# Out-projection of a decoder step as three fp32r products in place of one fp32 product

## The reference

```python
q, k, v, g = in_projection(rms_norm(yp, norm1_g[l]), w_in[l])
attn = merge_branches([banded_branch(q, k, v, dil, win // dil) for win, dil in DILATIONS])
c = conformer_conv(g_hist, conv_w[l], conv_b[l], conv_ln_g[l], conv_ln_b[l])
yp = yp + jnp.concatenate([attn.astype(yp.dtype), c], axis=-1) @ w_out[l]     # the out-projection
yp = channel_block(yp, norm2_g[l], w_query[l], sub_keys1[l], sub_keys2[l], expert_u[l], expert_v[l])
...
y_prompt = rms_norm(yp, final_g)
```

## Time and profile before

| what | value |
|---|---|
| median of 3 runs | 1710.42 us (1708.64 to 1710.57) |
| the profiled execution, its time | 1709.66 us |
| the profiled execution, its span | 1707.8 us |
| PE busy | 1645.9 us, 96% of the span |
| DVE busy | 1316.1 us, 77% |
| ACT busy | 618.3 us, 36% |
| mean granted TensorE clock | 0.99 of full |

### The profile page before, as it was taken

One profiled execution on the slowest core, in us unless ns is written; L12 is line 12 of the kernel. 1 busy time (PEld: TensorE's weight loads), 2 busy tenths in 40 slices (PEclk: granted clock), 3 DMA queues, 4 the chain that ended last, 5 costly groups with the idle time before them and its releaser, 6 DMA issues.

```text
span 1707.8 us, 24171 instructions
## 1 busy us (share of the span) xinstructions
PE 1645.9 (96%) x8587; PEld 1373.7 (80%) x8587; DVE 1316.1 (77%) x2697; ACT 618.3 (36%) x1034; POOL 484.3 (28%) x511
## 2 busy tenths in 40 slices
PE   7998988999999999987999999999999999999998
PEld 6777664467777669976999999999999999998886
DVE  5788463247898879976888788888888888889976
ACT  5322452221111158862333333333333333333434
POOL 1000000011223300013444444444444444445420
PEclk9999999999999999998999999999999999999999
DMA  8312813032221127888999999999999999999883
GB/s 283 121 69 71 312 66 118 0 140 75 75 74 50 62 80 221 255 269 298 339 349 353 331 347 356 336 338 357 339 337 352 351 336 342 361 336 356 329 313 140
DMA packets 164427, 411.53 MB, mean 241 GB/s; under 512 B 15503, under 2 KB 76461, under 8 KB 162893
## 3 DMA queue, kind: packets, MB, share of 16 engines
q1 hardware_dynamic: 118229, 242.20, 41.2%
q0 software_dynamic: 46080, 167.79, 26.6%
HBM read 375.34 MB, written 33.24 MB: 239 GB/s over the span
## 4 chain that ended last, share of the span: by engine, by line
PE 78%; DVE 2%; DMA 1%; SPq 1%; ACT 1%; issue 0%; DVEq 0%; ACTq 0%
PE bank L1471 30%; PE bank L1423 25%; PE bank L1410 7%; PE bank L1362 7%; PE bank L1340 3%; PE bank L1452 3%; PE bank L1399 1%; DVE placed L1934 1%; DMA u<-in_uT 1%; SPq L1285 1%; DMA gates_kept<-staged 1%; DVE hot_b L1927 0%; DVE here L1930 0%; DVE h_low L1911 0%; PE bank L1332 0%; ACT qh L1525 0%
## 5 line engine op out<-in xcount | busy, mean ns | idle before, releaser
L1471 PE MATMUL bank<-v_parts,p_high 128*128 128x512 f32 x1404 | 434.7, 391 | 2.4 <-DVE p_low L1911 2.4
L1679 POOL DMA_INDIRECT rows<-in_u_rows,row_u x160 | 198.2, 1239 | 399.5 <-DVE dots L1967 219.9
L1471 PEld LDWEIGHTS bank<-v_parts,p_high 128*128 128x128 f32 x1404 | 262.4, 188 | 51.5 <-issue 3.5
L1423 PE MATMUL bank<-h_high,u_high 128*128 128x384 f32 x832 | 282.7, 340 | 10.6 <-DVE u_low L1911 9.9
L1423 PE MATMUL bank<-h_low,u_high 128*128 128x384 f32 x832 | 283.0, 340 | 0.0
L1679 POOL DMA_INDIRECT rows<-in_v,row_u x160 | 212.9, 1331 | 239.4 <-DVE y L1977 170.5
L1423 PE MATMUL bank<-h_high,u_low 128*128 128x384 f32 x832 | 278.7, 335 | 0.0
L1471 PE MATMUL bank<-v_parts,p_low 128*128 128x512 f32 x702 | 273.6, 390 | 0.0
L1911 DVE TENSOR_TENSOR u_low<-u,u_high 128x1024 fp32r<-128x1024 f32 x115 | 140.8, 1224 | 146.7 <-ACT u_high L1560 146.4
L1596 ACT CAST p_high<-gel 128x384 fp32r<-128x384 f32 x128 | 65.8, 514 | 380.6 <-DVE gel L1955 363.5
L1423 PEld LDWEIGHTS bank<-h_high,u_high 128*128 128x128 f32 x832 | 157.0, 189 | 14.8 <-DVE u_low L1911 10.4
(11 more groups left out here) (235 smaller groups left out, 2440.2 us busy)
## 6 DMA issues: line engine op xcount, KB each, us to landing
vv<-in_v SPq DMA_DIRECT2D x117, 512.0 KB, 5.4
u<-in_uT SPq DMA_DIRECT2D x104, 512.0 KB
gate<-gates_kept SPq DMA_DIRECT2D x30, 768.0 KB, 8.3
gates_kept<-staged SPq DMA_DIRECT2D x11, 2048.0 KB, 9.7
early<-in_uT SPq DMA_DIRECT2D x24, 512.0 KB, 3.6
w_in_sb<-in_w_in SPq DMA_DIRECT2D x9, 1024.0 KB, 8.6
wq<-in_w_q SPq DMA_DIRECT2D x16, 512.0 KB, 3.7
ckT<-in_ckT SPq DMA_DIRECT2D x4, 1536.0 KB, 14.5
```

The lines of the kernel that those rows point to most:

```text
L1423: ins = pe.matmul(a_ps[par][:, 0:DT], x[:, par, k], y, start=(k == 0 and n == 0), stop=(k == KT - 1 and n == 2))
L1471: ins = pe.matmul(y_ps[2 * (i - 1) + half][:], x[:, b, of], y[:, part], start=(t == 0 and n == 0), stop=(t == NK - 1 and n == 2))
L1679: nc.gpsimd.indirect_dma_start(rows[:, r % ROW_BUFS], None, table, bass.IndirectOffsetOnAxis(ap=row_u[:, s_:s_ + 1], axis=0)).then_inc(fet ...
```

## The change

For the four prompt tiles the fp32 product catT·wo becomes three fp32r products: high·high, high·low and low·high. ACT and DVE make the parts at the head of the stage, one k-slice of 1024 columns after another: ACT rounds `wo[:, k]` into `wo_high[k]`, DVE subtracts into `wo_low[:, k]`. The heads of tile i are split in two half-tiles of four k-slices: `cat_high` has two buffers, `cat_low` is written over `catT`. Tiles 0 and 1 are split at the head, tiles 2 and 3 between the steps of the tiles before. Tile 0 is projected with k outside and n inside, so that PE can start on the first k-slice; tiles 1 to 3 keep the order n, k.

The samples' product stays fp32. It moves from the end of the out-projections to their front, into bank 7; ACT copies it out into `joint` at once. Turn 1, which uses bank 7, waits for that copy.

```diff
+            def out_samples():
+                for k in range(KT):
+                    for g in range(4):
+                        ins = pe.matmul(banks[7][32 * g:32 * g + NS, 0:D // 4], catT[:, k, cols(4)],
+                                        wo[:, k, g * D // 4:(g + 1) * D // 4], start=(k == 0), stop=(k == KT - 1))
+                ins.then_inc(samples_outed, 1)
+
+            def out_part(i, n, k):
+
+                if i == 0 and n == 0:
+                    pe.wait_ge(o_split, k + 1)
+                if n == 0 and k % 4 == 0:
+                    pe.wait_ge(cat_split, 2 * i + k // 4 + 1)
+                part = slice(n * 512, (n + 1) * 512)
+                for z, (x, y) in enumerate(((cat_high[:, i % 2, k], wo_high[k]), (cat_high[:, i % 2, k], wo_low[:, k]),
+                                            (cat_low[:, k, cols(i)], wo_high[k]))):
+                    ins = pe.matmul(banks[2 * (i % 2) + n][:], x, y[:, part], start=(k == 0 and z == 0),
+                                    stop=(k == KT - 1 and z == 2))
+                return ins
+
             def out_projection(i):
-                if i == 4:
-                    wait(pe, added, 2 * i - 3)
+
+                if i == 0:
                     for k in range(KT):
-                        for g in range(4):
-                            ins = pe.matmul(banks[0][32 * g:32 * g + NS, 0:D // 4], catT[:, k, cols(i)],
-                                            wo[:, k, g * D // 4:(g + 1) * D // 4], start=(k == 0), stop=(k == KT - 1))
-                    ins.then_inc(outed, 2)
+                        for n in range(2):
+                            ins = out_part(i, n, k)
+                            if k == KT - 1:
+                                ins.then_inc(outed, 1)
                     return
                 for n in range(2):
-                    b = 2 * (i % 2) + n
                     wait(pe, added, 2 * i + n - 3)
                     for k in range(KT):
-                        ins = pe.matmul(banks[b][0:ROWS[i]], catT[:, k, cols(i)], wo[:, k, n * 512:(n + 1) * 512],
-                                        start=(k == 0), stop=(k == KT - 1))
+                        ins = out_part(i, n, k)
                     ins.then_inc(outed, 1)
...
+                    if i == n == 1:
+                        pe.wait_ge(joined, 1)
...
             pe.wait_ge(wo_in, 16)
+            out_samples()
             for i in range(TILES + 1):
-                if i < TILES:
+                if i < TILES - 1:
                     out_projection(i)
...
+            def round_cat(i, n):
+                if i >= 2:
+                    act.wait_ge(outed, 2 * (i - 1))
+                k = slice(4 * n, 4 * n + 4)
+                nc.scalar.copy(cat_high[:, i % 2, k], catT[:, k, cols(i)]).then_inc(cat_rounded, 1)
+
+            act.wait_ge(wo_in, 16)
+            for k in range(KT):
+                if k < 2:
+                    round_cat(0, k)
+                nc.scalar.copy(wo_high[k][:], wo[:, k]).then_inc(o_rounded, 1)
+            for n in range(2):
+                round_cat(1, n)
+            act.wait_ge(samples_outed, 1)
+            for g in range(4):
+                ins = nc.scalar.copy(joint[0:NS, g * D // 4:(g + 1) * D // 4], banks[7][32 * g:32 * g + NS, 0:D // 4])
+            ins.then_inc(joined, 1)
             for i in range(TILES):
                 r = ROWS[i]
+                if i in (1, 2):
+                    for n in range(2):
+                        round_cat(i + 1, n)
...
-            pool.wait_ge(outed, 2 * TILES)
+            pool.wait_ge(outed, 2 * TILES - 2)
+            pool.wait_ge(samples_outed, 1)
...
+            def split_cat(i, n):
+                dve.wait_ge(cat_rounded, 2 * i + n + 1)
+                k = slice(4 * n, 4 * n + 4)
+                nc.vector.tensor_tensor(cat_low[:, k, cols(i)], catT[:, k, cols(i)], cat_high[:, i % 2, k].bitcast(F32),
+                                        ALU.subtract).then_inc(cat_split, 1)
+
+            for k in range(KT):
+                if k < 2:
+                    split_cat(0, k)
+                dve.wait_ge(o_rounded, k + 1)
+                nc.vector.tensor_tensor(wo_low[:, k], wo[:, k], wo_high[k][:].bitcast(F32), ALU.subtract).then_inc(o_split, 1)
+            for n in range(2):
+                split_cat(1, n)
             dve.wait_ge(x_in, 32)
...
             for i in range(TILES):
                 r = ROWS[i]
+                if i in (1, 2):
+                    for n in range(2):
+                        split_cat(i + 1, n)
                 for n in range(2):
                     half = slice(n * 512, (n + 1) * 512)
                     if i == 4:
                         dve.wait_ge(joined, 1)
-                        more = xr[0:r, 0, half]
+                        more = joint[0:r, half]
```

More of the change, by code:

```diff
@@ L1068, in route @@
         iota_f = base("iota_f", [P, NK])
+        h_at = base.at
         h_high = base("h_high", [P, KT, DT], F32R)
@@ L1099, in route @@
         keysT = sb("keysT", [P, 2, NK])
+        iota = sb("iota", [P, TOPK])
+        place = sb("place", [P, TOPK, TOPK], BF16)
+        spreads = sb("spreads", [P, PACK, NS])
+        over = Region(nc, sb.at, s.wo_at)
+        wo_low = over("wo_low", [P, KT, D], F32R)
+        wo_high = [*(over(f"wo_high{k}", [P, D], F32R) for k in range(KT - 2)),
+                   *(nc.alloc_sbuf_tensor_at(f"wo_high{k}", [P, D], F32R, offset=s.wo_at + (k + 2) * D * 4)
+                     for k in range(KT - 2, KT))]
+        joint = over("joint", [P, D])
+        cat_low = nc.alloc_sbuf_tensor_at("cat_low", [P, KT, T], F32R, offset=s.catT_at)
+        cat_high = nc.alloc_sbuf_tensor_at("cat_high", [P, 2, KT, P], F32R, offset=h_at)
         qh = sb("qh", [P, 4, T])
@@ L1110, in route @@
         hit = sb("hit", [P, 2, TILES, TOPK, TOPK], BF16)
-        place = sb("place", [P, TOPK, TOPK], BF16)
-        iota = sb("iota", [P, TOPK])
         keyf = sb("keyf", [P, 2, 2, TILES, TOPK])
@@ L1118, in route @@
         row_f = sb("row_f", [P, FETCHED])
-        spreads = sb("spreads", [P, PACK, NS])
         banks = [ctx.enter_context(nc.psum_tensor(f"bank{b}", [P, 512], F32)) for b in range(8)]
@@ L1152, in route @@
         wq_in = [sem(f"wq_in{b}") for b in range(4)]
-        outed, joined, added, squared, meaned = (sem(x) for x in ("outed", "joined", "added", "squared", "meaned"))
+        o_rounded, o_split, cat_rounded, cat_split = (sem(x) for x in ("o_rounded", "o_split", "cat_rounded", "cat_split"))
+        samples_outed, outed, joined, added, squared, meaned = (sem(x) for x in ("samples_outed", "outed", "joined", "added", "squared", "meaned"))
         rooted, inverted, scaled = sem("rooted"), sem("inverted"), sem("scaled")
@@ L1502, in _ @@
                     act.wait_ge(h0_ready, 1)
[L1503 to L1508, removed]
                 act.wait_ge(added, 2 * (i + 1))
```

## The result

| | median us | runs |
|---|---|---|
| before | 1710.42 | 1708.64 to 1712.12, 5 runs |
| after | 1701.10 | 1700.53 to 1703.20, 5 runs |

The ratio is 0.9949, with a 95% interval of 0.9938 to 0.9961: 8.7 us faster by the ratio, 9.3 by the medians. Forecast were 1701.6 us (1698.0 to 1705.8), a gain of 8.8. Timed again later beside other kernels, it took 1701.93 us (1697.56 to 1703.67, 5 runs) against 1711.03, ratio 0.9940 (0.9925 to 0.9956).

The account below looks back on a forecast made before the run. The prediction took PE's matmuls to bound the stage. A spread product 9.8 us sooner, less 1.0 for the clock, gave 8.8: 1709.66 became 1700.9, and with the median 0.8 higher 1701.6 us, range 1698.0 to 1705.8.

Parts of the forecast that it names:

- A tile on PE: Out-projection: 48 fp32r products at 0.227 us, 10.9 to 11.2 us a tile against 13.73; four tiles save 11.3 us.
- The rule of 131 ns: Skill's spacing of 512-column matmuls in a stream, 6.3 us a tile; the prediction went by the trace's 227 ns.
- The splits cost nothing: At the stage's head, splits hide behind samples and tile 0's products: slice 7 ready at 11.5 us, wanted at 15.0.
- The path: PE from samples through tiles and turns to the spread product, which starts at 343.7 against 353.43, 9.8 us sooner.
- The clock: New 2.9 us of idle PE before turn 3 may bring half clock, losing 1.5 us; 1.0 us was taken.
- sign of over 7 us below full: PE's clock below full for over 7 us in the changed stage would show the prediction wrong.
- The check of the sum: Stage's gain re-added: 11.3 products, plus 3.6 samples, less 2.9 idle, 1.7 half clock and what hid behind turn 3 and query.
- Behind the spread product: After the changed stage, everything moves as a whole; the distance from the spread product to the end stays unchanged.
- A: Low clock 3.4 us longer at the head and two falls in the tail: gain about 5, 1705.4 us; chance 0.12.
- B: Later DMA wait of 12.58 us for an expert tile takes up to all the gain: 1707 to 1711; chance 0.07.
- C: In tile 0 the splits pace PE: slower from 3.1 us a slice, 1716 us at 3.5; chance 0.04.
- D: Out-projection products come at 0.19 us instead of 0.227: gain 17.6, about 1692 us; chance 0.01.

Follow-up runs that it names:

- Double_split: The kernel after with a second, unused subtraction on DVE before each weight slice; stage 68.64 us, 1704.00 us (1 run).
- n_outer: The kernel after with tile 0 in the order of the other tiles, n outside and k inside; stage 64.07 us, 1703.82 us (1 run).
- after_again: The kernel after, unchanged, run once more for a second profile; stage 61.43 us, 1699.30 us (1 run).
- after_timed: The kernel after, unchanged, timed again beside other kernels; stage 63.87 us, median 1701.93 us (5 runs).
- paired: The kernel after with wo_low[k] and wo_high[k] side by side in memory for the first six slices; 1702.74 us (1 run).
- fp32_samples_first: The kernel after with the prompt tiles as fp32 products and no splits, samples still in front; stage 71.78 us, 1711.92 us (1 run).
- samples_last: The kernel after with the samples' product back at the end of the out-projections, splits left at the head; stage 63.06 us, median 1700.63 us (5 runs).
- keep_warm: The kernel after with 11 unused products in PE's wait before turn 3; 1697.55 us (1 run), timed again 1699.00 us (5 runs).

## Why the prediction was right, point by point

- **A tile on PE** was to take 10.9 to 11.2 us and took 11.16 to 11.2: 0.233 us a product, not 0.227. This is the one term that was mis-sized: 4 x 0.26 = 1.1 us of the stage. The prediction gives a distance other than 0.227 as a sign of being wrong, and this sign is met. I took the expert loop's 512-column rows as the nearest. The trace of before has a nearer stage, the in-projection, with the same shape in the same three-product form, 0.23 to 0.24 us apart (timeline of before; I hadn't looked there):

```profile
18.52 0.39 PE L659 MATMUL proj<-w_low,x_high 128*128 128x512 f32 x1
18.75 0.39 PE L659 MATMUL proj<-w_high,x_low 128*128 128x512 f32 x1
18.98 0.40 PE L659 MATMUL proj<-w_high,x_high 128*128 128x512 f32 x1
19.22 0.39 PE L659 MATMUL proj<-w_low,x_high 128*128 128x512 f32 x1
```

- **The rule of 131 ns** (the Trainium skill, TensorE: Matmul & The Clock Gate, Back-to-back issue gap) does not hold here: 192 products at 0.233 us.
- **The splits cost nothing**: right. Slice 7 was there 11.4 us in (forecast 11.5), samples done after 5.35 (5.5; 5.3 to 6.2 over the profiles, as the low clock covers more or less of them). Double_split and n_outer priced the slack.
- **The path**: by the chain, the spread product 60.3 us behind the start without a further fall of the clock and 61.8 with it. With the products at 0.233 instead of 0.227 this is 61.4 and 62.9; measured were 61.43 (after_again) and 62.84 (after). In after_timed it was 63.87: there the samples took 6.19 us, 0.8 more.
- **The clock**: the fall in turn 3 and the first query was named, at 1.5 us; it cost 1.4 where it came. That the dip of before at 357 might be replaced by it was named too; in fact the profiles have both (four), the first alone (one) or none (two), so that up to 3.1 us hang on it. At the head the low clock lasted 3.4 us in some profiles with the samples in front and 5.2 in others. The prediction's sign of over 7 us below full in the stage is met in three of those seven (after_timed, n_outer, paired: 8.6 us), and not in the profile after (6.8). I took 1.0 us as a mean of unlike cases, which was lucky more than known: that the median came out within 0.5 us of the forecast is partly this luck.
- **The check of the sum** does not hold, though the path does. It booked 3.6 us for the samples as cover of the splits and took off 1.7 for the half clock. But the samples cost the same work at the head as near the end, and before had its low clock at the head too (1.9 us, on tile 0). By the path's own numbers the products give 11.3, the tail 2.0 (11.46 with the samples in it, 9.5 without) and the clock at the head 0.1, and the samples at the head take 3.6: 9.8 again. In fp32_samples_first the move alone lost 1.7 us, and samples_last shows that the other order pays nearly the same in another place.
- **Behind the spread product** no time was given back, as forecast. From head 0's last query to the span's end the profiles of the kernels have 1336.5 to 1340.3 us, before 1339.5, after 1338.1. The two with fp32 tiles (before and fp32_samples_first) are among the three longest; whether a microsecond of the gain lies there, two profiles can't tell.
- **The rivals**: A (the clock costs more) came in part. The clock fell twice behind tile 3 in the profile after, with 7.2 us of gain in the stage instead of 8.8; in after_timed the longer low clock at the head came on top, with 6.2. The medians stayed below A's 1705.4. B did not come: the wait for the expert tile ended 411.7 us behind head 0 in the profile after, and 412.1 in the one of before, so its end moved with the rest. C and D did not come either (1.14 us a slice, 0.233 us a product).

## What to carry to other kernels

Three fp32r products cost 3 x 0.233 us where an fp32 product of 128x128 by 128x512 costs 0.858, so the form saves 19% of such products' time on PE (a tile took 11.16 us instead of 13.73), if another engine's splits hide behind work that PE has anyway; count what the last slice needs against PE's pace. When work is moved to cover one gap, look at the gap that it leaves: here each place cost about the same. When two profiles are compared for a microsecond, compare the clock in each stretch first: here the same kernel's stage varied by 2.4 us, nearly all of it by the clock. For a term's price look for the same instruction form in every stage of the trace, and take the stage that resembles the new one, not the costliest.

## What the runs showed of the hardware

- The granted clock differs between executions of one kernel with the same idle time of PE: 2.95 us of idle was followed by the lower level in five profiles of seven, at a cost of 1.4 us in the profile after, and in four of them by a second fall that cost 1.7 us in the next queries. In the profile after the clock fell while PE was still idle. Unused products in the gap went with full clock in both profiles of keep_warm and with a narrower spread of the times (1697.25 to 1699.44 against 1697.56 to 1703.67); that they caused it is favoured, not shown. In double_split waits of 0.6 us, one in each 2.3, left the clock at 1.00.
- The clock rose from the lower level to the full one at 289.5 in the profile after, while PE ran only the samples' narrow products (32 columns of weights in four column groups): about 30 of their 64 records ran at half pace (5.35 us in all against 3.63).
- fp32r products of one shape came 0.233 us apart in two stages and 0.227 in the expert loop; in the out-projection another place of the weights' parts in memory (paired) changed nothing.
